# Opening of a recurrent mixer: low-rank products from the norm's output, roundings on ScalarE, weight remainders by parity

## What is computed

```python
xx = shift(h) - h                               # shift: one token back, zero ahead
xs = h[None] + xx[None] * mu[:, None, None, :]  # six mixes, of r, k, v, w, a, g
r, k, v = xs[0] @ W_r, xs[1] @ W_k, xs[2] @ W_v           # 1024 x 1024 each
decay = exp(-exp(-softplus(-(w0 + tanh(xs[3] @ w_la) @ w_lb)) - 0.5))
a = sigmoid(a0 + (xs[4] @ a_la) @ a_lb)                   # ranks 64 and 64
g = sigmoid(xs[5] @ g_la) @ g_lb                          # rank 128
kk = heads(k * k_k); kk = kk / max(sqrt(sum(kk * kk)), 1e-12)
k = k * (1 + (a - 1) * k_a)
y = wkv7_scan(r, decay, k, v, kk, kk * a)                 # chunks of 64 tokens
```

## Time and profile before

| | us |
|---|---|
| median of 3 runs | 1251.37 |
| the profiled execution | 1249.6 |
| its span | 1247.5 |
| TensorE busy (share of the span) | 1085.5 (87%) |
| its weight loads | 917.6 (74%) |
| VectorE | 493.3 (40%) |
| ScalarE | 444.3 (36%) |
| GpSimd | 496.3 (40%) |

### The profile page before, as it was taken

The page is one execution under the profiler, slowest core; times in us unless marked ns, Lnnn a source line. Parts: engine busy times, 40 slices in busy tenths (PEclk is TensorE's granted clock), DMA queues, the critical chain, the costliest instruction groups (busy, mean ns, idle before and its releaser), DMA issues.

```text
span 1247.5 us, 22101 instructions
## 1 busy us (share of the span) xinstructions
PE 1085.5 (87%) x9538; PEld 917.6 (74%) x9548; DVE 493.3 (40%) x755; ACT 444.3 (36%) x550; POOL 496.3 (40%) x112
## 2 busy tenths in 40 slices
PE   6999999999969769999988999999999586666675
PEld 5899889989949658899877998998977453333332
DVE  2153230101174765242246887887343531111113
ACT  5454353444434241222145343445643321111112
POOL 4878758787833264400251633543742000000000
PEclk9999999999989889699988999998999688788777
DMA  9755556556531240000227778868535459999992
GB/s 360 230 178 183 166 174 186 183 183 200 187 103 56 83 152 35 2 3 4 70 68 295 291 268 321 336 252 270 170 135 186 172 238 420 422 422 421 423 421 97
DMA packets 99126, 260.90 MB, mean 209 GB/s; under 512 B 6368, under 2 KB 61024, under 8 KB 83184
## 3 DMA queue, kind: packets, MB, share of 16 engines
q1 hardware_dynamic: 93728, 249.78, 54.5%
q10 hardware_dynamic: 5328, 10.09, 2.3%
HBM read 258.80 MB, written 1.05 MB: 208 GB/s over the span
## 4 chain that ended last, share of the span: by engine, by line
issue 29%; PE 28%; POOL 21%; DMA 15%; DVE 4%; ACT 2%; SPq 1%; another core or an unknown queue 1%; POOLq 0%; DVEq 0%; ACTq 0%
POOL wlo L550 21%; DMA w_e<-in_w_expert_down 14%; PE ps L1800 3%; PE ps L1802 3%; PE ps L1801 3%; PE ps L2546 2%; PE ps L2135 2%; PE ps L2144 2%; PE ps L2148 1%; DMA raw<-in_sgu_w_in 1%; PE ps L1872 1%; PE ps L2060 1%; SPq L506 1%; PE ps L2243 1%; PE ps L2474 1%
## 5 line engine op out<-in xcount | busy, mean ns | idle before, releaser
L550 POOL TENSOR_TENSOR wlo<-raw,whi 128x2048 fp32r<-128x2048 f32 x99 | 473.5, 4796 | 438.0 <-ACT whi L599 431.4
L1800 PE MATMUL ps<-Hh,whi 128*128 128x256 f32 x832 | 240.7, 289 | 9.3 <-POOL wlo L550 4.4
L599 ACT ACTIVATE whi<-raw 128x2048 fp32r<-128x2048 f32 x116 | 220.0, 1909 | 56.2 <-DMA raw<-in_ffn_w 27.8
L1802 PE MATMUL ps<-Hh,wlo 128*128 128x256 f32 x832 | 238.6, 287 | 0.0
L1801 PE MATMUL ps<-Hl,whi 128*128 128x256 f32 x832 | 238.5, 287 | 0.0
L1800 PEld LDWEIGHTS ps<-Hh,whi 128*128 128x128 f32 x832 | 163.0, 196 | 13.6 <-POOL wlo L550 5.9
L1801 PEld LDWEIGHTS ps<-Hl,whi 128*128 128x128 f32 x832 | 163.0, 196 | 0.7 <-issue 0.2
L1802 PEld LDWEIGHTS ps<-Hh,wlo 128*128 128x128 f32 x832 | 162.9, 196 | 0.0
L2519 PE MATMUL ps<-w_e,arena 128*32 128x256 f32 x1024 | 88.9, 524 | 62.1 <-DMA w_e<-in_w_expert_gate 33.1
L2519 PEld LDWEIGHTS ps<-w_e,arena 128*32 128x32 f32 x1024 | 41.6, 149 | 107.3 <-issue 38.7
L1800 PE MATMUL ps<-whi,Fh 128*128 128x512 f32 x256 | 99.8, 390 | 0.0
(11 more groups left out here) (373 smaller groups left out, 1707.7 us busy)
## 6 DMA issues: line engine op xcount, KB each, us to landing
raw<-in_ffn_w SPq DMA_DIRECT2D x64, 1024.0 KB, 5.6
w_e<-in_w_expert_gate SPq DMA_DIRECT2D x32, 1024.0 KB, 18.1
w_e<-in_w_expert_up SPq DMA_DIRECT2D x32, 1024.0 KB, 18.6
w_e<-in_w_expert_down SPq DMA_DIRECT2D x32, 1024.0 KB, 20.6
arena<-in_w_ada SPq DMA_DIRECT2D x24, 1024.0 KB, 10.2
raw<-in_sgu_w_in SPq DMA_DIRECT2D x16, 1024.0 KB, 7.4
raw<-in_rwkv_w_rkv SPq DMA_DIRECT2D x12, 1024.0 KB, 5.1
raw<-in_sgu_w_out SPq DMA_DIRECT2D x8, 1024.0 KB, 5.0
```

The costliest lines, as they stand in the source:

```text
L550: pool.tensor_tensor(wlo[n % RING][:, :], raw[n % RING][:, :], whi[n % RING][:, :].bitcast(F32), ALU.subtract).then_inc(lo_done, 1)
L599: act.activation(whi[n % RING][:, :], raw[n % RING][:, :], ACT.Copy).then_inc(hi_done, 1)
L1800: pe.matmul(o, sh, mh, start=start, stop=False, skip_group_check=True)
L1802: return pe.matmul(o, sl, mh, start=False, stop=stop, skip_group_check=True)
```

## The change

1. *Low-rank products.* In the first feed-forward's rounds, now written out on ScalarE instead of in a loop, six small activations per round make scaled weights: mu * weight (in a second slot, r_la_past) and (1 - mu) * weight (in place). The products down then take h itself and h shifted by one token, which accumulate in one bank: 8 k x 2 products for w and a together (128 columns), the same for g, each k as soon as ScalarE's gain is there. VectorE's three mixes for w, a and g go. The products up alternate between w and a, into banks 4 to 7 and 0 to 3.
2. *Splitting the mixed inputs.* ScalarE rounds the mixed input by quarters (`high`), VectorE only subtracts (`low`). For r and v `high` waits for the last use of the operand before.
3. *Remainders of weights by parity.* From k's first piece to v's last, GpSimd makes the even ones and VectorE the odd ones (`weight_low`).
4. *k's followers.* ScalarE makes k * k_k and its square from PSUM, and 1 + (a - 1) k_a with an affine activation. The sums of squares stand after r's first piece on TensorE, the spreading of the reciprocal after r's third. The middle of the low-rank products, r and the exponential get slots of their own.

```diff
@@ remainders: which semaphore counts a piece @@
+            if n < MIX:
+                return lo_done, n + 1
+            if n < MIX_OUT:
+                return (lo_vector, (n - MIX) // 2 + 1) if n % 2 else (lo_done, MIX + (n - MIX) // 2 + 1)
@@ GpSimd @@
-            with pool.Fori(1, FIRST["rwkv_o"] // RING) as i:
+            with pool.Fori(1, MIX // RING) as i:
                 for n in range(RING):
                     lo(n, i)
+            for n in range(MIX, MIX_OUT, 2):
+                lo(n)
@@ ScalarE, first feed-forward @@
+                for i in range(ROUNDS):
                     step(i)
+                    if i == 0:
+                        act.wait_ge(sem("lora_in"), 80)
+                        act.wait_ge(sem("lora_mid"), 2)
+                    for at, w, p in ((0, 64, 3), (64, 64, 4), (128, 128, 5)):
+                        now, past = r_la[:, i, at:at + w], r_la_past[:, i, at:at + w]
+                        act.activation(past, now, ACT.Copy, scale=mu[:, 8 * p + i:8 * p + i + 1])
+                        ins = act.activation(now, now, ACT.Copy, scale=one_less[:, 8 * p + i - 24:8 * p + i - 23])
+                    ins.then_inc(sem("lora_weights"), 1)
@@ ScalarE, mixer @@
+                hi(MIX + 3)
+                def high(p):
+                    if p:
+                        act.wait_ge(used, MIX + 4 * p)
+                    for q in range(4):
+                        act.wait_ge(sem("xs"), 4 * p + q + 1)
+                        act.activation(Hh[:, 512 * q:512 * (q + 1)], slot(4)[:, 512 * q:512 * (q + 1)], ACT.Copy
+                                       ).then_inc(sem("xs_hi"), 1)
+                high(0)
...
+                def k_copies(c):
+                    act.wait_ge(used, MIX + c + 1)
+                    src = ps[:, 4 + c, :].rearrange("p (f n) -> p f n", f=2)
+                    act.activation(r_k[:, 2 * c:2 * c + 2, :], src, ACT.Copy)
+                    for f in range(2):
+                        j = 2 * c + f
+                        act.activation(r_kk[:, j, :], src[:, f, :], ACT.Copy, scale=colv("k_k", j))
+                        ins = act.activation(r_squares[:, j, :], src[:, f, :], ACT.Square, scale=colv("k_k", j))
+                    ins.then_inc(sem("rwkv_copied"), 1)
+                    hi(MIX + c + 4)
...
+                for c in range(3):
+                    k_copies(c)
+                high(1)
+                k_copies(3)
+                act.wait_ge(sem("cum_excl"), 1)
+                act.activation(slot(5), slot(5), ACT.Exp, scale=-KAPPA).then_inc(sem("decay"), 1)
                 act.wait_ge(sem("kk_sum_mm"), 1)
                 act.activation(r_norm, ps[0:HEADS, 3, 0:SEQ], ACT.Sqrt).then_inc(sem("root"), 1)
...
+                for c in range(3):
+                    r_copies(c)
+                high(2)
+                r_copies(3)
@@ VectorE, mixer (after the differences) @@
+                def low(p):
+                    for q in range(4):
+                        at = slice(512 * q, 512 * (q + 1))
+                        dve.wait_ge(sem("xs_hi"), 4 * p + q + 1)
+                        dve.tensor_tensor(Hl[:, at], slot(4)[:, at], Hh[:, at].bitcast(F32), ALU.subtract
+                                          ).then_inc(sem("xs_low"), 1)
...
+                mix(0, 1)
+                dve.wait_ge(sem("xs"), 4)
+                low(0)
+                weight_low(MIX + 1)
+                weight_low(MIX + 3)
+                mix(1, 0)
...
+                weight_low(MIX + 5)
+                low(1)
+                mix(2, 2)
+                weight_low(MIX + 7)
...
+                weight_low(MIX + 9)
...
+                low(2)
+                dve.wait_ge(sem("lora_sigmoid"), 8)
+                dve.tensor_tensor(slot(10), slot(10), slot(7), ALU.mult).then_inc(sem("b_done"), 1)
+                weight_low(MIX + 11)
@@ TensorE, mixer @@
+                pe.wait_ge(sem("lora_weights"), KT)
+                for bank, c in ((2, slice(0, 128)), (3, slice(128, 256))):
+                    for k in range(KT):
+                        if bank == 2 and k % 2 == 0:
+                            pe.wait_ge(sem("norm_hi"), 4 * 2 + k // 2 + 1)
+                        pe.matmul(ps[:, bank, 0:SEQ], r_la[:, k, c], r_h[:, k, :], start=k == 0, stop=False,
+                                  skip_group_check=True)
+                        ins = pe.matmul(ps[:, bank, 1:SEQ], r_la_past[:, k, c], r_h[:, k, 0:SEQ - 1], start=False,
+                                        stop=k == KT - 1, skip_group_check=True)
+                    ins.then_inc(sem("lora_mm"), 1)
+                pe.wait_ge(sem("lora_mid"), 4)
+                for q in range(4):
+                    if q == 3:
+                        pe.wait_ge(sem("g_sigmoid"), 1)
+                    for j in (2 * q, 2 * q + 1):
+                        for m in range(2):
+                            rows = slice(64 * m, 64 * (m + 1))
+                            ins = pe.matmul(ps[:, 4 * (1 - m) + q, 256 * (j % 2):256 * (j % 2 + 1)],
                                             r_lb[rows, P * j:P * (j + 1)], r_mid[rows, :], start=True, stop=True)
+                    ins.then_inc(sem("lora2_mm"), 1)
```

More of the change, by code:

```diff
@@ L722, in rwkv @@
[L722 to L726, removed]
+                act.activation(gsig, ps[:, 3, 0:SEQ], ACT.Sigmoid).then_inc(sem("g_sigmoid"), 1)
+                for m, (dst, bias) in enumerate(((r_sg, "w0"), (r_a, "a0"))):
                     for q in range(4):
-                        act.wait_ge(sem("lora2_mm"), (4 if what == "a" else 0) + q + 1)
+                        act.wait_ge(sem("lora2_mm"), q + 1)
@@ L729, in rwkv @@
                         for j in (2 * q, 2 * q + 1):
-                            ins = act.activation(dst[:, j, :], ps[:, 4 + q, 256 * (j % 2):256 * (j % 2 + 1)],
+                            ins = act.activation(dst[:, j, :], ps[:, 4 * (1 - m) + q, 256 * (j % 2):256 * (j % 2 + 1)],
                                                  ACT.Sigmoid, bias=colv(bias, j))
                         ins.then_inc(sem("lora_sigmoid"), 1)
[L734 to L744, removed]
-                        if FIRST[name] + c + AHEAD < FIRST["rwkv_o"]:
-                            hi(FIRST[name] + c + AHEAD)
@@ L748, in rwkv @@
-                copies("rwkv_k", r_k)
+                act.dma_start(r_headrows, a["head_rows"]).then_inc(sem("headrows_in"), 16)
+                def k_copies(c):
[8 more added lines that the diff above has]
+                    hi(MIX + c + 4)
@@ L756, in rwkv @@
                 act.wait_ge(sem("rinv_mm"), 4)
                 act.dma_start(r_gb, a["rwkv_g_lora_b"][0]).then_inc(sem("headrows_in"), 16)
-                act.wait_ge(sem("tmp_free"), 1)
-                act.activation(slot(4), slot(6), ACT.Exp, scale=KAPPA).then_inc(sem("decay"), 1)
+                act.wait_ge(sem("xs"), 12)
+                act.activation(slot(1), slot(6), ACT.Exp, scale=KAPPA).then_inc(sem("decay"), 1)
+                act.wait_ge(sem("b_done"), 1)
+                for j in range(KT):
+                    ins = act.activation(r_a[:, j, :], r_a[:, j, :], ACT.Identity, scale=colv("k_a", j),
+                                         bias=one_less[:, 24 + j:25 + j])
@@ L760, in rwkv @@
+                ins.then_inc(sem("a_new"), 1)
                 act.wait_ge(sem("decay"), 2)
                 act.activation(slot(6), slot(6), ACT.Exp, scale=-KAPPA).then_inc(sem("decay"), 1)
-                copies("rwkv_v", r_v)
+                for half in range(2):
+                    act.wait_ge(used, MIX + 8 + 2 * half + 2)
+                    for t in range(TT):
+                        act.activation(r_v[:, t, 512 * half:512 * (half + 1)], ps[:, 4 + 2 * half + t, :], ACT.Copy
+                                       ).then_inc(sem("rwkv_copied"), 1)
@@ L2007, in rwkv @@
[L2007 to L2018 removed]
+                    pe.wait_ge(sem("lora_sigmoid"), c + 1)
@@ L2019, in rwkv @@
+                    feature_tiles(n, 4 + c, HhT, HlT, mixed_ready(0) if c == 0 else None).then_inc(used, 1)
                 for c in range(4):
```

185 lines of the change are left out of this document (78 added, 107 removed).

## The result

| | us |
|---|---|
| before, median of 4 runs beside it | 1251.22 |
| changed, median of 4 runs (1211.5 to 1215.2) | 1212.72 |
| ratio, with its 95% interval | 0.9699 (0.9679 to 0.9719) |
| profiled execution of the changed kernel, its span | 1211.91, 1210.1 |

The kernel before has two groups of runs with the same code, 1234.6 to 1244.3 us (32 of 76 runs, median 1239.2) and 1248.3 to 1254.2 us (44 of 76, median 1249.9), and the runs that the forecast started from were of the upper one. From the median of before's lower group that is 27.2 us, from that of its upper one 37.9.

The account below looks back on a forecast made before the run. TensorE's waits and low clock in the mixer's opening were taken as the bound; the terms summed to 99.4 us, 100.1 with handovers, against 127.9, a gain rounded to 27.5: 1223.9 us, range 1219 to 1233.

Parts of the forecast that it names:

- Bounds, and what moves up as a whole: TensorE busy 103.1 of the mixer opening's 127.9 us, 24.8 us of waits; everything after the opening moves up unchanged.
- Clock: Opening, after the change: 2.5 us lost to TensorE's low clock, bounds 0 and 8; before it lost about 11 us.
- Feed-forward rounds: Six small ScalarE scalings per round, at most 2.3 us, fit in 9.28 us of idle time and cost nothing.
- Products down: Start of the opening: 64 instructions on TensorE at full clock without waits, 13.4 us.
- Up: Low-rank products up, after those down: alternating 64-row halves overlap nearly twofold, 4.0 us, bounds 3.2 and 6.4.
- k to r: TensorE's gap between k's and r's pieces: GpSimd's remainder shuts VectorE's subtraction out, 3.7 us, lower bound 1.3.
- r to v: TensorE's gap between r's and v's pieces: rounding and first subtraction, 1.3 us, where it cost 8.3 before.
- r with the 16-row products: r's four pieces, 23.0 us, plus two sets of 16 instructions between them, 6.8 us, without waits.
- Behind it: VectorE's scaled operands, 20.4 us from v's first product, are covered by v's 21.7 and the bonus products' 3.5 us.
- Rival 1: Gaps and low clock take back more and the 64-row halves don't overlap: gain 19.6, 1231.8 us; chance 0.26.
- rivals 3 and 4: 3: ScalarE's scalings delay feed-forward rounds, 1294 us, chance 0.05; 4: something later absorbs the gain, 1251 us, chance 0.03.
- Rival 2: VectorE isn't shut out between k and r and the clock holds: gain 32.4, 1219.0 us; chance 0.06.

Follow-up runs that it names:

- the second profile: The changed kernel itself, unchanged, profiled once more: opening 100.05 us, and 664.0 us for all that follows the chunk inversion.

## Why the prediction was wrong, point by point

- *Bounds, and what moves up as a whole.* Here it failed. The sentence was that what follows the opening "waits for events of this same program and for no fixed time, so I take it to move up as a whole". The order of events did move up as a whole; its speed didn't stay: 24 us of the chunk inversion stood at half clock in the execution that I summed against, and the same work ran at full clock in the profiles of the changed kernel (and by their times in all ten of its runs), 10.4 us. The windows of the prediction end at 465 us. One behind them shows 0.51 over 24 us with TensorE busy throughout, and so a price that a run can win or lose. The *Clock* term should have had that stretch: not in the sum, but as a rival of -10 us, down to about 1213. Of the 9.9 us between the forecast span of 1220.0 and the measured 1210.1 this stage is 10.4; the diagonal is 2.45 on the same side, the opening (1.05), the chunk matrices (0.3) and what follows (1.6) are on the other. Why the inversion falls in some executions, and in none of the changed kernel as it stands, stays open.
- *What a measurement can tell.* The prediction took 0.2% for it. The same code's runs reach from 1234.6 to 1254.2 us, 1.6%, in two groups; three runs of one group don't show that.
- *Feed-forward rounds.* As forecast: 22.40 us each, with 11.3 instead of 9.8 us of ScalarE. What I missed stood 2.5 us behind the last one's products, the diagonal that took 3.54 us beside GpSimd's third remainder: 2.45 us. I had used the rule that the two exclude each other where the change adds such a meeting and not looked for one that it takes away.
- *Products down:* 13.75 us (13.4). *Up:* 3.8 (4.0), the overlap of halves shown by its reversal. *k:* 23.05 (23.0). *k to r:* 3.45 (3.7), its cause shown. *r to v:* 1.5 (1.3). *v:* 22.0 (21.7). *r with the 16-row products:* 33.9 from 397.4 to 431.3, where 29.8 was forecast; 3.4 of it is low clock (1.7 at r's start, 1.7 behind the 16-row products), where the *Clock* term had 2.5, and the two sets of 16-row products took 3.6 and 3.7 us, not 3.4. The sum was 100.1, the stage took 101.45, and 100.05 in the second profile.
- *What the parity was credited with.* "The 2.3 us wait for GpSimd goes with the parity" named the wrong cause: the wait is gone with all twelve remainders on GpSimd as well. What is left is that ScalarE's copies, and the roundings behind them, no longer wait for VectorE's new k.
- *Behind it.* The scaled operands were ready at 453.6, 20.8 us after v's first product (20.4), 1.2 us before v's last: no cost. The terms that the prediction lists for it add up to 19.7, not 20.4; nothing hung on that.
- *The gain against like runs.* 27.5 forecast; 27.2 between the medians of the changed kernel and of before's lower group. That it comes so close is in part luck: the errors inside it, 2.45 us more gained ahead of the opening, 1.3 less in it than the sum of 100.1 said, and 1.6 in later stages (which is scatter), nearly cancel. The account of the opening was right but for the parity, and the missing term is the clock of a stage that the change doesn't touch.
- *Rivals.* Rival 1 had the opposite sign; rivals 3 and 4 didn't come. Rival 2, VectorE not shut out, gave a time of the right side for a wrong reason.

## What to carry to other kernels

Before summing a change, list the granted clock of the whole span, not only of the stage that is changed: a long stretch at half clock with TensorE busy is time that the next execution may not show, and a single profile doesn't say how often it is there. Compare runs of like clock, stage by stage (one run here had the upper group's mean clock and time without the fall), and put a dozen runs of each kernel beside each other, before a difference of one per cent is given to a cause. And look for VectorE's small instructions on SBUF operands beside GpSimd's long ones: the 0.29 us diagonal took 3.5 us, the 0.69 us subtraction 4.86, so the first of them to move is the one on TensorE's path.

## What the runs showed of the hardware that I had not expected

- A busy TensorE can stay at half clock for 24 us: 403 instructions, nearly all on quarter arrays, in 24.1 us, all of it busy, at clock 0.51. The same work begun at full clock stayed at full clock for its 68 us.
- Adding work can take the slower group of runs away: four thin products (0.9 us) ahead of the stage took the kernel before from 7 upper runs of 13 beside them to none of ten, three dense products in an empty wait from 18 of 29 to none of twelve. It doesn't carry over: the same four products made one run in five of the changed kernel fall.
- Products with 64 columns take the time of those with 2 (3.68 against 3.6 us for 16), and the first steps of the stage behind them ran at full clock instead of 0.67; the clock fell some 7 us into the stage instead.
- The Trainium skill (TensorEngine Tiling (Array Packing), Key Properties) says that different tiles multiply in parallel; the pair of 64-row halves took 3.7 instead of 6.42 us for 32 fp32 instructions, 0.5 us short of the full factor of two.
